# Attention products of probabilities and values with one head's high and low value columns side by side, in a fused encoder layer on one Trainium2 core

## The reference

```python
def sliding_window_sink_attention(q, k, v, t5_tab, sinks):    # branch B: 8 heads, 2 heads of keys and values
    ...
    p = jax.nn.softmax(jnp.concatenate([s, sink], axis=-1), axis=-1)[..., :band]
    o = jnp.einsum('bcgrqk,bckgd->bcqgrd', p.astype(v.dtype), vb)

def chunk_band_attention(q, k, v, rel_tab):                    # branch C: 8 heads
    ...
    p = jax.nn.softmax(s, axis=-1)
    o = jnp.einsum('bchqk,bckhd->bcqhd', p.astype(v.dtype), vb)
```

## Time and profile before

| | |
|---|---|
| median of 3 runs | 888.55 us |
| the profiled execution | 889.22 us |
| its span in the trace | 887.4 us |
| PE busy | 875.4 us (99%) |
| DVE, ACT, POOL busy | 388.7, 395.0, 451.9 us (44, 45, 51%) |
| granted TensorE clock, mean | 0.996 |
| unit 6 (C), from one first slot's softmax to the next | 178.3 to 203.5 us, PE busy 25.20 of 25.20 us, DVE 15.80, ACT 16.36 |

### The profile page before, as it was taken

One profiled execution on the slowest core, in us unless ns is written; L12 is line 12 of the kernel. 1 busy time (PEld: TensorE's weight loads), 2 busy tenths in 40 slices (PEclk: granted clock), 3 DMA queues, 4 the chain that ended last, 5 costly groups with the idle time before them and its releaser, 6 DMA issues.

```text
span 887.4 us, 13120 instructions
## 1 busy us (share of the span) xinstructions
PE 875.4 (99%) x4316; PEld 737.7 (83%) x4316; DVE 388.7 (44%) x815; ACT 395.0 (45%) x684; POOL 451.9 (51%) x628
## 2 busy tenths in 40 slices
PE   9999999999999999999999899999999999999997
PEld 7888888888888888888888689888888888888886
DVE  5677777666555623222231355444444444200004
ACT  5566656676555643333332435444444444311112
POOL 4554443323333447666666636555555555555551
PEclk9999999999999999999999899999999999999999
DMA  7442222232222223332337303333333332322202
GB/s 226 141 119 64 79 84 70 82 94 56 75 78 78 61 70 97 106 96 87 102 116 240 116 27 94 96 95 96 100 101 101 97 95 95 118 95 95 95 24 96
DMA packets 131999, 85.61 MB, mean 96 GB/s; under 512 B 6808, under 2 KB 121440, under 8 KB 131957
## 3 DMA queue, kind: packets, MB, share of 16 engines
q1 hardware_dynamic: 130906, 81.34, 30.5%
q10 hardware_dynamic: 1050, 3.72, 1.2%
HBM read 82.89 MB, written 2.14 MB: 96 GB/s over the span
## 4 chain that ended last, share of the span: by engine, by line
PE 73%; POOL 13%; issue 9%; DVE 2%; DMA 1%; ACT 1%; SPq 0%; POOLq 0%; DVEq 0%; ACTq 0%
PE banks L1264 22%; PE banks L1266 22%; PE banks L1265 22%; POOL ring_lo L537 12%; PE banks L1422 2%; PE banks L1344 1%; PE banks L1343 1%; DMA scratch<-in_x_dram 1%; POOL pages L545 1%; PE banks L1394 1%; DVE scratch L1188 1%; PE banks L1355 0%; DVE u_lo L918 0%; PE banks L1283 0%; DMA ring_raw<-in_w_ffn_up_dram 0%
## 5 line engine op out<-in xcount | busy, mean ns | idle before, releaser
L537 POOL TENSOR_TENSOR ring_lo<-ring_raw,ring_hi 128x256 fp32r<-128x256 f32 x560 | 419.9, 781 | 379.8 <-ACT ring_hi L641 379.7
L1264 PE MATMUL banks<-u_hi,ring_hi 128*128 128x512 f32 (+1 forms) x768 | 300.5, 391 | 0.3 <-DVE u_lo L918 0.3
L1266 PE MATMUL banks<-u_hi,ring_lo 128*128 128x512 f32 (+1 forms) x768 | 296.1, 385 | 0.0
L1265 PE MATMUL banks<-u_lo,ring_hi 128*128 128x512 f32 (+1 forms) x768 | 295.6, 385 | 0.0
L641 ACT CAST ring_hi<-ring_raw 128x1024 fp32r<-128x1024 f32 x140 | 145.8, 1043 | 137.0 <-PE banks L1266 129.8
L1266 PEld LDWEIGHTS banks<-u_hi,ring_lo 128*128 128x128 f32 x768 | 144.2, 188 | 29.6
L1264 PEld LDWEIGHTS banks<-u_hi,ring_hi 128*128 128x128 f32 x768 | 144.4, 188 | 27.6 <-DVE u_lo L918 0.5
L1265 PEld LDWEIGHTS banks<-u_lo,ring_hi 128*128 128x128 f32 x768 | 144.5, 188 | 27.2
L1229 DVE SCALAR_TENSOR_TENSOR wide<-banks,cols,wide 128x511 f32<-128x511 f32 x88 | 65.9, 749 | 102.2 <-ACT wide L871 96.1
L1264 PE MATMUL banks<-ring_hi,pages 128*128 128x512 f32 x240 | 94.9, 395 | 0.1
L1265 PE MATMUL banks<-ring_lo,pages 128*128 128x512 f32 x240 | 94.2, 392 | 0.0
(11 more groups left out here) (138 smaller groups left out, 1030.1 us busy)
## 6 DMA issues: line engine op xcount, KB each, us to landing
ring_raw<-in_w_ffn_up_dram SPq DMA_DIRECT2D x88, 256.0 KB, 3.1
ring_raw<-in_w_in_dram SPq DMA_DIRECT2D x60, 256.0 KB, 3.4
ring_raw<-in_w_gate_dram SPq DMA_DIRECT2D x48, 256.0 KB, 3.1
ring_raw<-in_w_ffn_down_dram SPq DMA_DIRECT2D x44, 256.0 KB, 2.9
ring_raw<-in_w_out_dram SPq DMA_DIRECT2D x16, 256.0 KB, 3.1
scratch<-in_x_dram SPq DMA_DIRECT2D x4, 512.0 KB, 5.8
ring_raw<-in_w_proj_a_dram SPq DMA_DIRECT2D x8, 256.0 KB, 2.8
ring_raw<-in_w_proj_c_dram SPq DMA_DIRECT2D x8, 256.0 KB, 3.2
```

Of the source, the lines that this page charges most:

```text
L537: last = pool.tensor_tensor(wlo[:, r, c], raw[:, r, c], whi[:, r, c].bitcast(F32), ALU.subtract)
L1264: pe.matmul(out, lhs_hi, rhs_hi, start=start, stop=False)
L1265: pe.matmul(out, lhs_hi, rhs_lo, start=False, stop=False)
L1266: return pe.matmul(out, lhs_lo, rhs_hi, start=False, stop=stop)
```

## The change

The high and low values of one head stand side by side. `v_parts` writes V so that of each block of keys and each head 64 high columns are followed by 64 low ones, and a stationary operand of 128 columns is now [high | low] of one head.

In **B** both heads of a unit share their values, so the two matmuls of a block are [high | low] by the two heads' high probabilities and [high | low] by their low probabilities. The product's first 64 partitions are (all probabilities by high values), the other 64 (all probabilities by low values). That includes low by low, which the kernel before left out. `y_high` takes the first half as the high part; `y_low` has four operations for two: two subtract the high part from the second half into `v_feat` (`rest`), two add the first half.

In **C** there is one matmul for each head and block: its [high | low] values by its high and low probabilities side by side (256 columns). The result comes in four parts, of which three are added: ACT copies the one of low probabilities by high values out (`y_copy_c`, 64x256, into a page of `scratch`), DVE adds the one of high probabilities by low values and then the one of high by high (`y_sum_c`, two operations of 64x256), ACT takes the high part of the sum (`y_high_c`, two copies of 64x128) and DVE the low part (`y_low_c`, two of 64x128, from SBUF). This is done in every slot, two slots after the one it belongs to, and the banks alternate by slot.

```diff
+def v_parts(u):
+    pair = pages[:, v_page(u, 0):v_page(u, 0) + 2, :]
+    if u < 4:
+        return pair[:, 0, :], pair[:, 1, :]
+    flat = pair.rearrange("p a n -> p (a n)").rearrange("p (g a d) -> p g a d", a=2, d=CHUNK)
+    return flat[:, :, 0, :], flat[:, :, 1, :]
+def turned_v(u):
+    src = psum[:, turn_bank(u), :]
+    return src if u < 4 else src.rearrange("p (g d) -> p g d", d=CHUNK)
 def q_page(u, m):
...
 def y_count(u, half):
...
+def y_bank_c(s):
+    bank = psum[:, O_BANK + s % 2, :].rearrange("p (m a n) -> p m a n", m=2, a=2)
+    return bank[0:CHUNK, :, 0, ::-1], bank[0:CHUNK, :, 1, ::-1], bank[CHUNK:P, :, 0, ::-1]
+def y_spare(s):
+    page = scratch[0:CHUNK, YTOK_PAGE + s % 2, :].rearrange("p (i m n) -> p i m n", i=2, m=2)
+    return page[:, 0], page[:, 1]
 def y_parts(u, half):
     out = []
+    bank = psum[:, O_BANK + half, :].rearrange("p (t m n) -> p t m n", t=2, m=2)[:, :, :, ::-1]
     for m in range(2):
-        src = m if branch(u) == "C" else (u - 8) // 2
-        bank = psum[CHUNK * src:CHUNK * (src + 1), O_BANK + half, :].rearrange("p (t m n) -> p t m n", t=2, m=2)
-        out.append((bank[:, :, m, ::-1], slice(CHUNK * m, CHUNK * (m + 1)),
+        out.append((bank[0:CHUNK, :, m], bank[CHUNK:P, :, m], slice(CHUNK * m, CHUNK * (m + 1)),
                     slice(2 * P * half, 2 * P * (half + 1))))
...
         act.wait_ge(pv_done, s + 1)
-        for src, rows, to in y_parts(u, qt // 2):
+        for src, _, rows, to in y_parts(u, qt // 2):
             last = act.copy(pages[rows, Y_HI + u, to].rearrange("p (t n) -> p t n", t=2), src)
+        last.then_inc(y_hi, 1)
+    def y_copy_c(s):
+        act.wait_ge(pv_done, s + 1)
+        if s == 4 * TT + 1:
+            act.wait_ge(y_turned, 4)
+        if s >= 4 * TT + 2:
+            act.wait_ge(y_sum, s - 2 - 4 * TT + 1)
+        act.copy(y_spare(s)[0], y_bank_c(s)[1]).then_inc(y_copied, 1)
+    def y_high_c(s):
+        u, qt = divmod(s, TT)
+        act.wait_ge(y_sum, s - 4 * TT + 1)
+        for m in range(2):
+            last = act.copy(pages[half_rows(m), Y_HI + u, qt * P:(qt + 1) * P], y_spare(s)[1][:, m])
         last.then_inc(y_hi, 1)
...
             y_high_a(u - 1)
+        if 4 * TT <= s - 2 < 8 * TT:
+            y_copy_c(s - 2)
         split_now = [t for t in range(RING, T_ATT + RING) if split_slot(t) == s]
...
                 act.wait_ge(pv_done, TT * (u - 1))
-            act.copy(pages[:, v_page(u, 0), :], psum[:, turn_bank(u), :]).then_inc(v_hi, 1)
+            act.copy(v_parts(u)[0], turned_v(u)).then_inc(v_hi, 1)
         for t in split_now[1:]:
                 proj_out(g)
-        if s > 4 * TT and qt % 2 == 0:
+        if 4 * TT <= s - 2 < 8 * TT:
+            y_high_c(s - 2)
+        if s > 8 * TT and qt % 2 == 0:
             y_high(s - 1)
...
         dve.wait_ge(y_hi, y_count(u, qt // 2))
-        for src, rows, to in y_parts(u, qt // 2):
-            hi, lo = (pages[rows, page + u, to].rearrange("p (t n) -> p t n", t=2) for page in (Y_HI, Y_LO))
-            last = dve.tensor_tensor(lo, src, hi.bitcast(F32), sub)
+        rest = v_feat[:, 0:2 * P].rearrange("p (t n) -> p t n", t=2)
+        for _, by_v_lo, rows, to in y_parts(u, qt // 2):
+            hi = pages[rows, Y_HI + u, to].rearrange("p (t n) -> p t n", t=2)
+            dve.tensor_tensor(rest[rows], by_v_lo, hi.bitcast(F32), sub).then_inc(y_rest, 1)
+        dve.wait_ge(y_rest, 2 * (y_count(u, qt // 2) - 4 - 4 * TT))
+        for by_v_hi, _, rows, to in y_parts(u, qt // 2):
+            lo = pages[rows, Y_LO + u, to].rearrange("p (t n) -> p t n", t=2)
+            last = dve.tensor_tensor(lo, by_v_hi, rest[rows], ALU.add)
+        last.then_inc(y_lo, 1)
+    def y_sum_c(s):
+        dve.wait_ge(y_copied, s - 4 * TT + 1)
+        by_hi, _, by_v_lo = y_bank_c(s)
+        rest, total = y_spare(s)
+        dve.tensor_tensor(rest, by_v_lo, rest, ALU.add).then_inc(y_part, 1)
+        dve.wait_ge(y_part, s + 1)
+        dve.tensor_tensor(total, by_hi, rest, ALU.add).then_inc(y_sum, 1)
+    def y_low_c(s):
+        u, qt = divmod(s, TT)
+        dve.wait_ge(y_hi, y_count_c(s))
+        to = slice(qt * P, (qt + 1) * P)
+        for m in range(2):
+            last = dve.tensor_tensor(pages[half_rows(m), Y_LO + u, to], y_spare(s)[1][:, m],
+                                     pages[half_rows(m), Y_HI + u, to].bitcast(F32), sub)
         last.then_inc(y_lo, 1)
...
             y_tok(s - 1)
-        if s > 4 * TT and qt % 2 == 0:
+        if 4 * TT <= s - 2 < 8 * TT:
+            y_low_c(s - 2)
+        if 4 * TT <= s - 1 < 8 * TT:
+            y_sum_c(s - 1)
+        if s > 8 * TT and qt % 2 == 0:
             y_low(s - 1)
...
             dve.wait_ge(v_hi, u + 1)
-            dve.tensor_tensor(pages[:, v_page(u, 1), :], psum[:, turn_bank(u), :],
-                              pages[:, v_page(u, 0), :].bitcast(F32), sub).then_inc(v_lo, 1)
+            dve.tensor_tensor(v_parts(u)[1], turned_v(u), v_parts(u)[0].bitcast(F32), sub).then_inc(v_lo, 1)
         if qt == 2 and 1 <= u <= 4:
...
             pe.wait_ge(v_lo, u + 1)
-        vh, vl = v_page(u, 0), v_page(u, 1)
+        vh = v_page(u, 0)
         if branch(u) == "A":
                 pe.wait_ge(y_out, s - 1)
-        elif u == 4:
+        elif s < 4 * TT + 2:
             pe.wait_ge(y_out, 4 * TT)
+        elif s < 8 * TT:
+            pe.wait_ge(y_sum, s - 2 - 4 * TT + 1)
+        elif u == 8 and qt % 2 == 0:
+            pe.wait_ge(y_sum, 4 * TT - 1 + qt // 2)
         elif qt % 2 == 0:
             pe.wait_ge(probs_cleared, 1)
...
+        v_flat = pages[:, vh:vh + 2, :].rearrange("p a n -> p (a n)")
+        last_b = len(blocks) - 1
+        def probs_b(b, first, step, n=2):
+            return pages[:, PT_PG + first:PT_PG + first + step * (n - 1) + 1:step, b * P:(b + 1) * P]
...
-                mm = triple(psum[:, O_BANK + qt // 2, 2 * P * (qt % 2):2 * P * (qt % 2 + 1)],
-                            v_hi_b, v_lo_b, pages[:, PT_PG:PT_PG + 2, pc],
-                            pages[:, PT_PG + 2:PT_PG + 4, pc], b == 0, b == len(blocks) - 1)
+        elif branch(u) == "C":
+            for m in range(2):
+                for b, (kt, _, _) in enumerate(blocks):
+                    c = 2 * P * kt + P * m
+                    mm = pe.matmul(psum[:, O_BANK + s % 2, 2 * P * m:2 * P * (m + 1)], v_flat[:, c:c + P],
+                                   probs_b(b, m, 2), start=b == 0, stop=b == last_b)
+        else:
+            for b, (kt, _, _) in enumerate(blocks):
+                c = 2 * P * kt + P * ((u - 8) // 2)
+                for part in range(2):
+                    mm = pe.matmul(psum[:, O_BANK + qt // 2, 2 * P * (qt % 2):2 * P * (qt % 2 + 1)],
+                                   v_flat[:, c:c + P], probs_b(b, 2 * part, 1),
+                                   start=b == 0 and part == 0, stop=b == last_b and part == 1)
         mm.then_inc(pv_done, 1)
...
             if i is None:
-                pe.wait_ge(y_lo, y_count(UNITS - 1, 1) if c == 3 else y_count(8, 0) - 1)
+                pe.wait_ge(y_lo, y_count(UNITS - 1, 1) if c == 3 else y_count_c(8 * TT - 1))
             for h, br in enumerate(branches):```

The order on two engines shows where the new steps stand; both pieces are of slot 21 (unit 5, qt 1) and of what follows it.

ACT before, from `probs_high(20)` to the K of slot 22 (`waits` are the semaphores waited for):

```order
L730 CAST pages<-banks 128x2x128 [waits pv_done,probs_turned]
L765 ACTIVATE scratch,rowsum<-scratch,negmax 128x256 [waits biased] x2
L686 ACTIVATE pages<-banks 64x512 [waits scores,tile_used]
L686 ACTIVATE pages<-banks 64x512 x3
L730 CAST pages<-banks 128x2x256 [waits pv_done,probs_turned]
L765 ACTIVATE scratch,rowsum<-scratch,negmax 128x384 [waits biased] x2
L641 CAST ring_hi<-ring_raw 128x1024 [waits raw_loaded2,tile_used]
L750 CAST pages<-banks 64x256 [waits pv_done]
L750 CAST pages<-banks 64x256
L695 CAST pages<-banks 64x512 [waits scores,tile_used]
```

21 lines of the change are left out of this document (11 added, 10 removed).

## The result

The changed kernel took **896.55 us** (median of 4 runs, 896.13 to 897.26) beside 888.65 us for the one before in the same comparison (888.24 to 889.99): ratio 1.0087, 95% interval 1.0071 to 1.0103, 7.9 us slower. The forecast was 890.2 us, in a range from 886.0 to 895.0. The profiled execution's span is 894.8 us (before 887.4), its mean granted clock 0.996 as before.

What follows compares the result with a forecast made beforehand. PE was taken as the bound, busy 875.4 of 887.4 us, with a nearly closed ring of DVE, ACT and PE. C +4.9 and B -3.3 made +1.6 us on 888.55: 890.2 us, range 886.0 to 895.0.

Steps and rivals of the forecast that it cites:

- PE's saving: Attention stage, C and B: one of three products per key block goes, 0.119 us each, 8.1 us in all.
- the ring: Attention slots: DVE, ACT and PE pass probabilities round in strict order; nearly closed already, 0.4 us of room at V's transposes.
- B: Attention stage B: gains 3.3 us on PE; no wait charged for two more low-part operations every second slot.
- Prices of the added operations: C, each slot from 18 to 33: y_sum_c 0.88 us, y_low_c 0.60, y_high_c 2 x 0.264, y_copy_c 0.37.
- My own bound of 1.4: C, DVE: upper bound in us for the y_low_c pair, from slower SBUF operations seen while POOL worked.
- The walk of unit 5: C, slots 21 to 24 step by step: PE waits of 0.4, 0.3, 1.3 and 0.9 us, 2.9 a unit.
- the net 1.7: C, per unit: 2.9 us of waits against 1.2 saved, +1.7; taken as +1.6 for units 5 and 6 each.
- Unit 4 at 0: C's first unit: new work begins in its third slot; two waits (0.35 and 0.8 us) eat its 1.2: 0 net.
- Unit 7: C's last unit: slot 30's wait grows from 0.49 to 2.2 us, then 0.5 and 0.7; 2.9 more, +1.7 net.
- Together: Units 4 to 7 of C: costs +4.9 us where it should gain 4.8, nearly 10 us of new waits.
- a dearer ring: C: y_sum_c and y_high_c at upper prices, 0.15 us more each slot; 893 to 895 us, chance 0.20.
- The cover holds: C: ACT's wait for the sum costs nothing, PE gains the full 8.1 us; 880.5 us, chance 0.12.

Runs made afterwards that it cites:

- the first run: New layout and two products a key block in B only, C as in the kernel before: 886.39 us, ratio 0.9974 to that kernel.
- C alone: New layout in C only, B as in the kernel before the change: 897.59 us, ratio 1.0099 to that kernel.
- the trace without that wait: Changed kernel with the low part of y of A ahead of C's first sum in slot 18: median 894.93 us, profiled execution 896.45 us.
- the high part elsewhere: Changed kernel with ACT's high part one slot later and DVE's sum ahead of the low part of the block ahead: 884.10 us, ratio 0.9945.
- the low part behind V: Changed kernel, high part in the next slot, y of A's low part first in slot 18, C's low part behind V's: 881.86 us, the fastest.
- low part at the slot's end: Changed kernel with DVE's low part of C moved from in front of the sum to the slot's end: 888.18 us, ratio 0.9995 to before.
- in the last slots alone: Changed kernel with C's low part moved to the slot's end only in each unit's last slot (19, 23, 27, 31): 890.01 us, ratio 1.0017.

## Why the prediction was wrong

- **What bounds, and PE's saving: right.** 136 products for 204, 0.12 us apart; 8.1 us forecast, 7.7 less busy. With the ring opened, 6.7 of them reach the time.
- **B: right.** 3.3 forecast, 3.1 in the trace, no wait of PE behind slot 32, shown alone in the first run.
- **Prices of the added operations: right but for one.** `y_sum_c` took 0.88 us (181.15 to 182.03) for 0.88, beside POOL as well, `y_high_c` 0.61 for 0.53, a clear pair of `y_low_c` 0.58 for 0.60. Beside POOL I took 1.4 in the last slot of a unit (1.55) and the clear 0.60 in the first (1.17). My own bound of 1.4 wasn't applied there. C alone shows that step by itself: 0.59 us less wait in slot 20, and as much in the two units after it.
- **The walk of unit 5: right in all four places, short in size.** Forecast 0.4, 0.3, 1.3, 0.9 = 2.9; by starts 0.62, 0.59, 1.52, 1.29 = 4.0. Of the missing 1.1 us 0.16 at each wait (0.64) is what a wait costs beyond its idle (last section): a cost that the sum has no term for. The rest is mostly the pair in slot 24 (1.17 for 0.60). 0.2 us more came in the first distances behind the waits. Then I rounded the net 1.7 to 1.6, and it was +3.0 in units 5 and 6 each.
- **Unit 4 at 0: the step that failed most.** I judged it from two waits of 0.35 and 0.8; it lost 2.2 us. Its first V goes the same way as all others (waits 0.63 and 1.12 us in slot 20). I had also overlooked that the first sum stands ahead of `y_low_a(3)` in slot 18 (1.3 us). In the trace without that wait the one at `turn_v` is 1.36 instead of 0.63, and V's path alone makes the lag of 2.1 at slot 20.
- **Unit 7**: +1.7 forecast, +3.1 measured, with the wait of slot 30's probabilities at 2.2 as forecast. Behind it stood 0.48 us, and 0.26 and 1.18 at the first V of B, where I had 0.5 and 0.7.
- **Together**: C +11.2 for +4.9, of which unit 4 makes 2.2, units 5 and 6 2.8, unit 7 1.4.
- **The rival that came true** is the one of a dearer ring, and the upper end of the range was still 1.6 us short. Its mechanism (sum and high part at their upper prices) is not what happened; both cost what I had taken. The collision that I had bounded but not applied in the first slots, unit 4, and what each wait costs beyond its idle did it. "The cover holds" was wrong for this order of calls and nearly right for another: with the high part elsewhere 884 us, with the low part behind V 881.9, where that rival had said 880.5.
- **The range** counted prices as uncertain and the walk as settled. One unit was walked and three were judged from it; the 0 for unit 4 had no bound above it at all.

What stays open: what shifts POOL against DVE by the hundredth of a microsecond that decides a collision in C when only B differs, and whether that is also why two of the kernels (low part at the slot's end, and in the last slots alone) spread over 2.4 and 3.3 us from run to run, or whether that comes from ahead of slot 16, where the traces differ by 2.5 us; what decides whether the clock falls behind a wait; and the 1 us wait in slot 30, which the best version keeps.
